# The first chunk's solver steps: the ones inside a projection tile moved to the end of the tile before

## The reference, cut to what matters

```python
def gated_deltanet_mixer(h, w_in, conv_w, a_log, dt_bias, norm_g):
    proj = h @ w_in
    qkv = jax.nn.silu(causal_depthwise_conv(proj[..., :o1], conv_w))
    ...
    q = l2_normalize(qkv[..., :GDN_QK_W].reshape(b_sz, s_len, GDN_HEADS, GDN_DK))
    k = l2_normalize(qkv[..., GDN_QK_W:2 * GDN_QK_W].reshape(b_sz, s_len, GDN_HEADS, GDN_DK))
    o = gated_delta_rule_chunked(q, k, v, g, beta)

def gated_delta_rule_chunked(q, k, v, g, beta):
    lower = jnp.where(strict, jnp.einsum("bhncd,bhnkd->bhnck", kb, k) * decay, 0.0)
    rhs = jnp.concatenate([v * beta[..., None], kb * jnp.exp(gc)[..., None]], axis=-1)
    sol = lax.linalg.triangular_solve(lower, rhs, left_side=True, lower=True, unit_diagonal=True)
```

## Time and profile before

| | us |
|---|---|
| median of 3 runs | 2268.62 |
| lowest and highest | 2267.70, 2269.38 |
| the profiled execution, its own time | 2267.39 |
| its span, first to last instruction | 2265.5 |
| tiles 12 to 23 of the projection in it, 1014.6 to 1110.1 | 95.5 |

### The profile page before, as it was taken

One profiled execution on the slowest core, in us unless ns is written; L12 is line 12 of the kernel. 1 busy time (PEld: TensorE's weight loads), 2 busy tenths in 40 slices (PEclk: granted clock), 3 DMA queues, 4 the chain that ended last, 5 costly groups with the idle time before them and its releaser, 6 DMA issues.

```text
span 2265.5 us, 25512 instructions
## 1 busy us (share of the span) xinstructions
PE 2001.4 (88%) x9978; PEld 1541.7 (68%) x9978; DVE 1138.6 (50%) x1894; ACT 793.7 (35%) x1655; POOL 118.8 (5%) x85
## 2 busy tenths in 40 slices
PE   6977776988698776999998999999998999999997
PEld 5733433876465444878797788888875768888885
DVE  4577364645321112768555544554465745434444
ACT  3144444445121112663355332222342643222222
POOL 0000000000000002402132000000000000000000
PEclk9966787999799897899999999999998989999998
DMA  5100140333699997122200222223221012323320
GB/s 177 43 2 1 60 120 0 103 140 112 237 411 411 407 393 295 47 66 65 66 1 1 87 95 95 91 94 101 91 96 47 1 38 93 103 93 93 102 90 41
DMA packets 77383, 261.07 MB, mean 115 GB/s; under 512 B 9264, under 2 KB 11568, under 8 KB 76752
## 3 DMA queue, kind: packets, MB, share of 16 engines
q1 hardware_dynamic: 67104, 231.47, 28.6%
q0 software_dynamic: 5040, 19.58, 2.8%
q10 hardware_dynamic: 5120, 8.39, 1.0%
HBM read 242.62 MB, written 16.79 MB: 115 GB/s over the span
## 4 chain that ended last, share of the span: by engine, by line
PE 73%; DVE 12%; DMA 8%; ACT 4%; issue 2%; POOL 0%; SPq 0%; ACTq 0%; DVEq 0%; POOLq 0%
PE ps_pair L276 17%; PE ps_pair L278 17%; PE ps_pair L277 17%; DMA split_acts_as_f<-w_experts 6%; PE ps_pair L792 3%; PE ps_pair L1631 3%; PE ps_turn L2139 2%; PE ps_out L819 2%; PE ps_shared L819 2%; PE ps_turn L805 2%; DVE columns L895 1%; PE ps_pair L2139 1%; DMA w_raw<-w_mem 1%; DVE ps_pair L885 1%; DVE g L920 1%
## 5 line engine op out<-in xcount | busy, mean ns | idle before, releaser
L276 PE MATMUL ps_pair<-split_acts,w_high 128*128 128x512 f32 (+1 forms) x1824 | 717.0, 393 | 34.1 <-DVE split_acts L574 17.2
L277 PE MATMUL ps_pair<-split_acts,w_high 128*128 128x512 f32 (+1 forms) x1824 | 709.2, 389 | 0.0
L278 PE MATMUL ps_pair<-split_acts,w_low 128*128 128x512 f32 (+1 forms) x1824 | 708.7, 389 | 0.0
L237 DVE TENSOR_TENSOR w_low<-w_raw,w_high 128x1024 fp32r<-128x1024 f32 (+5 forms) x257 | 291.8, 1136 | 291.4 <-ACT w_high L231 289.6
L276 PEld LDWEIGHTS ps_pair<-split_acts,w_high 128*128 128x128 f32 x1824 | 345.9, 190 | 113.7 <-DVE w_low L237 29.8
L278 PEld LDWEIGHTS ps_pair<-split_acts,w_low 128*128 128x128 f32 x1824 | 345.4, 189 | 72.2
L277 PEld LDWEIGHTS ps_pair<-split_acts,w_high 128*128 128x128 f32 x1824 | 346.0, 190 | 69.0 <-issue 0.2
L231 ACT ACTIVATE w_high<-w_raw 128x1024 fp32r<-128x1024 f32 (+5 forms) x257 | 251.1, 978 | 235.3 <-PE ps_pair L278 201.9
L1631 PE MATMUL ps_pair<-split_acts_as_f 128*64 128x256 f32 x512 | 133.6, 420 | 39.2 <-DMA split_acts_as_f<-w_experts 34.8
L1633 PE MATMUL ps_pair<-split_acts_as_f 128*64 128x256 f32 x512 | 134.0, 421 | 0.0
L1631 PEld LDWEIGHTS ps_pair<-split_acts_as_f 128*64 128x64 f32 x512 | 75.0, 152 | 78.1 <-issue 51.9
(11 more groups left out here) (455 smaller groups left out, 2269.6 us busy)
## 6 DMA issues: line engine op xcount, KB each, us to landing
split_acts_as_f<-w_experts SPq DMA_DIRECT2D x192, 512.0 KB, 14.7
w_raw<-w_gu SPq DMA_DIRECT2D x88, 512.0 KB, 3.4
w_raw<-w_down SPq DMA_DIRECT2D x32, 448.0 KB, 3.2
w_raw<-w_gdnin SPq DMA_DIRECT2D x26, 512.0 KB, 3.4
w_raw<-w_out SPq DMA_DIRECT2D x24, 512.0 KB, 3.5
rows_y<-scratch ACTq DMA_DIRECT2D x64, 128.0 KB, 5.9
w_raw<-w_down SPq DMA_DIRECT2D x16, 512.0 KB, 3.5
w_raw<-w_in SPq DMA_DIRECT2D x15, 512.0 KB, 4.4
```

What stands on the lines that cost most here:

```text
L237: dve.tensor_tensor(WL[:, t % SPLIT, 0:kt * m], WRAW[:, t % RING, 0:kt * m], WH[:, t % SPLIT, 0:kt * m].bitcast(F32), ALU.subtract).then_i ...
L276: pe.matmul(out, wh[:, k, :], self.high(k), start=(k == 0), stop=False)
L277: pe.matmul(out, wh[:, k, :], self.low(k), start=False, stop=False)
L278: last = pe.matmul(out, wl[:, k, :], self.high(k), start=False, stop=(k == self.kt - 1))
```

## The change

Ten steps leave `middle` for the end of the tile before; each then stands directly behind the step that it depends on. Nothing is added or removed, and no instruction changes.

```diff
         at_tile(12, products(0, lambda q: last_turn))
         at_tile(13, turned_root(0, 0))
-        in_tile(14, step_u(0, 1))
+        at_tile(13, step_u(0, 1))
         at_tile(14, step_r(0, 1))
-        in_tile(15, turned_root(0, 1))
+        at_tile(14, turned_root(0, 1))
         at_tile(15, step_u(0, 2))
-        in_tile(16, step_r(0, 2))
+        at_tile(15, step_r(0, 2))
         at_tile(16, turned_root(0, 2))
-        in_tile(17, step_u(0, 3))
+        at_tile(16, step_u(0, 3))
         at_tile(17, query_norm(0, ps_o, key_squared(5)), step_r(0, 3))
-        in_tile(18, turned_root(0, 3))
+        at_tile(17, turned_root(0, 3))
         at_tile(18, On(tensor=lambda pe: need(pe, *mem0_out(1))), query_norm(1, ps_m, query_squared(0)), step_u(0, 4))
-        in_tile(19, step_r(0, 4))
+        at_tile(18, step_r(0, 4))
         at_tile(19, query_norm(2, ps_o, query_squared(1)), turned_root(0, 4))
-        in_tile(20, step_u(0, 5))
+        at_tile(19, step_u(0, 5))
         at_tile(20, query_norm(3, ps_m, query_squared(2)), step_r(0, 5))
-        in_tile(21, turned_root(0, 5))
+        at_tile(20, turned_root(0, 5))
         at_tile(21, query_norm(4, ps_o, query_squared(3)), step_u(0, 6))
-        in_tile(22, step_r(0, 6))
+        at_tile(21, step_r(0, 6))
         at_tile(22, query_norm(5, ps_m, query_squared(4)), rows_in(0, "KG", ps_s, lambda q: att_mem0.last))
-        in_tile(23, rows_in(0, "VR", ps_s, lambda q: ("c_dve", ("KG", 0, q))))
+        at_tile(22, rows_in(0, "VR", ps_s, lambda q: ("c_dve", ("KG", 0, q))))
```

## The result

The changed kernel takes 2277.64 us (median of 5 runs, 2277.36 to 2280.00) against 2268.62 (5 runs, 2266.85 to 2271.09): a ratio of 1.0041, with a 95% interval of 1.0027 to 1.0056, or 6 to 13 us. A second set of 5 runs gave 1.0036 (1.0022 to 1.0050). The profiled execution took 2277.64 us with a span of 2275.8, 10.3 longer than before.

What follows compares the result with a forecast made beforehand. TensorE's queue was taken to bound the stretch; waits of 8.9 us plus 1.7 for the clock gave 10.6 us on 2268.6, so 2279.2 us, range 2276.0 to 2282.4.

Steps and rivals of the forecast that it cites:

- Rival D: Tiles around 13: VectorE sets the pace, new waits replace ones coming anyway; no change, 2268.6 us; 5 in 100.
- R1 to T1: End of tile 14: VectorE's subtraction is in time since R1 starts 2.8 us later; wait of 0.67 us.
- T0 to U1: End of tile 13: U1 starts no earlier, half a tile of cover lost, 2.84 us; wait grows to some 5.5.
- The clock: TensorE behind U1's wait: slower passes cost 1.7 us, bounds 0 and 3.4; granted clock under 1 for 3 to 4 us.
- The nine joints: Ends of tiles 14 to 22: dependent steps directly behind each other, small waits of 0.2 to 1.3 us each.
- R to T: Ends of tiles 14, 17 and 20: transposes wait for VectorE's subtraction, 0.67 us each, 2.0 together.
- U to R: Tile 15, free ScalarE: wait of 0.23 us; tiles 18 and 21, behind a query norm: 0.58 each.
- T to U: End of tile 16: wait for the copy, 0.57 us; end of tile 19, behind a query norm: 1.26.
- Tiles that are cut no more: Uncut tiles save matmul kind changes, but joined steps lose about as much; 0, within 0.3 us either way.
- rival A: TensorE at tile 13: the waits come but the clock holds; 2277.5 us; 12 in 100.
- Rival B: VectorE falls behind through GpSimd, a late SiLU holds up a copy; two times 1.48 us more, 2282.2; 8 in 100.
- Rival C: Clock falls at each of the nine smaller waits too; 15.3 us on top, 2294.5; 4 in 100.

Runs made afterwards that it cites:

- the chain was moved: Kernel before with every step from U1 on moved half a tile later, no two steps joined; ratio 0.9994 (0.9985 to 1.0003).
- the kernels with U1 inside the tile: Changed kernel with U1 alone put back inside tile 14, ratio 1.0036; kernel before with only R and T joined (tiles 14, 17, 20), ratio 1.0015.
- the filled wait: Changed kernel with five idle matmuls on TensorE between T0 and U1; ratio 1.0035 (1.0022 to 1.0047).
- the kernel with U1 put back: Changed kernel with U1 alone put back inside tile 14; ratio to the kernel before 1.0036 (1.0023 to 1.0050).
- the second execution: Changed kernel run once more, nothing altered; ratio to the kernel before 1.0036 (1.0022 to 1.0050).
- the joints inside: Changed kernel with the joined steps of tiles 17 to 21 put, still joined, inside the next tile; ratio 1.0045 (1.0027 to 1.0063).
- the last kernel of the table: Kernel before with the chain half a tile later, GpSimd's identity addition behind U6, first mask behind tile 12's convolution; ratio 0.9991 (0.9982 to 1.0000).

## Why the prediction was right, point by point

- **The path.** TensorE's order sets this stretch from tile 15 on, as said. Not in tiles 12 to 14: there it is VectorE, with GpSimd at work beside it. Rival D was refused because no wait in the stretch could shrink; that was right for the sum of the changed kernel, but the lateness showed as soon as only a part was changed (R1 T1, 2.2 us) or the chain was moved (1.80 us at R1).
- **R1 to T1.** The forecast held that VectorE would be in time because R1 comes 2.8 us later; it was. It also read VectorE's lateness in the kernel before as "some 2 us", from the start of the taps, in front of which L2044 stands with 0.5 us. That leaves 1.5, and the kernels with U1 inside the tile showed 1.6.
- **T0 to U1.** 2.84 forecast, 2.70 measured (the filled wait). U1 came at the same distance from T0, the wait was 5.34 us against 5.5.
- **The clock.** 1.7 forecast, 2.3 measured, a term that came out too small. The forecast took the slow passes after one wait of 4.90 us. After a wait of the same 4.90 us at the same place the half clock lasted 3.4 us in the profiled execution of the kernel before and 6.8 in that of the kernel with U1 put back. Here it was 6.8, 4.85 of them with work, and not the 3 to 4 us that the prediction named as a sign. By the same subtraction (T0 to R1, less 10.39 and 2.70) the term was 2.5 in the second execution and 1.3 with the joints inside. The bounds of 0 to 3.4 held each time; that a single execution meets 1.7 would be luck.
- **The nine joints.** 6.0 forecast (the terms of the sum without the first), 6.2 measured as read from start to start: R to T 0.63 to 0.64 (0.67), U to R 0.26 (0.23) and 0.62 (0.58), T to U 0.66 (0.57) and 1.37 (1.26), KG to VR 0.77 (0.8).
- **Tiles that are cut no more.** Taken as 0 within 0.3; it was a gain of 1.0. From R1 to inner the changed kernel takes 76.56 us against 71.47, 5.1 more and not 6.2. In it the 24 matmuls of tiles 15 to 23 take 5.55 us a tile on the mean; in the kernel before, two halves take 5.67. Over nine tiles that is 1.0. This is the step of the prediction that failed: it had said that joined steps lose about as much as uncut tiles save.
- **The sum.** 10.6 forecast, 10.07 in the trace from T0 to inner and 10.3 in the span; 9.0 by the medians, whose interval, 6 to 13 us, holds both. The sum came out closer than its terms: the clock's 0.6 too little and the joints' 0.2 too little were made up for by 1.0 of uncut tiles and 0.1 of the half tile, which is luck. That 9.0 is close to rival A's 8.9 is no support for A: the clock fell. Rival B's 2282.2 stands as 2282.4 at the high end of the range; nothing hangs on the 0.2.
- **Rival B** did not occur: no SiLU held up a copy behind tile 13; VectorE's lateness shrank. **Rival C** did not either: from 1038.7 to 1119.6, with waits of up to 1.37 us from start to start, the granted clock was 1.00. The Trainium skill's rule on short idles between groups ("TensorE: Matmul & The Clock Gate", "A second HAM failure mode: psum-queue depth-cycling") is not borne out by waits of this length and distance. It would be too much to say that short waits never matter: see the last section for a wait of 2.23 us.

## What to carry to other kernels

Between two steps that hand over through another engine, some independent matmuls are worth the handover's time, 0.3 to 1.4 us here; half a tile (2.84 us) hid all nine of these. Look first for the place that already waits: cover taken away there costs nearly its full length (2.70 of 2.84 us), and when the wait of 2.65 us grew to 4.66 or 5.34, some 2.3 us of half clock came on top. When a wait ends at a chain of two engines, moving the waiting step only moves the wait; find the instruction that makes the chain late.

## What the runs showed of the hardware

VectorE's taps (two SBUF inputs, 128 by 512) took 0.78 us each alone, three of them 2.33; with one operation of GpSimd beside them three took 3.79 us, with two of them 5.25, and in the last kernel of the table the first instruction of a convolution (L2044) took 1.36 instead of 0.49 us beside GpSimd. The GpSimd operations beside these taps lasted 2.04 to 2.33 us each, and each cost VectorE some 1.5 us. The Trainium skill ("VectorE: DVE Perf Modes", section "Two Vector instructions with no wait between them") names a second read interface of SBUF that VectorE shares with GpSimd; moving GpSimd's work away gave the time back, which agrees with it and does not prove it.

Around tile 13 TensorE's clock fell to half after waits of 4.66, 5.34 and 5.35 us, and not after those of 1.20 and 2.65 us or with the wait filled; no run tried a length between 2.67 and 4.66 there. The length of a wait alone does not decide it. Behind the projection, in the kernel before, the clock went to half 1.0 us after the end of a wait of 2.23 us. TensorE's timeline and the table by stretch there:

```profile
1235.71 1.01 PE L2144 MATMUL ps_turn<-consts,split_acts_as_f 128*128 128x128 f32 x6 [2.23 <-DVE split_acts_as_f L2321]
1236.92 4.44 PE L2139 MATMUL ps_turn<-split_acts_as_f 128*128 128x128 f32 x24 [0.20 <-ACT split_acts_as_f L2286]
...
1236.70:1240.10 3.40, 3.21 (x16) 3.21 (x16) 1.25 (x2) 2.01 (x5) 0.00 (x0) 0.50 0.00 0
```

Why a wait of 2.23 us was followed by half clock there and one of 2.65 us at tile 13 was not, no run here shows.
